# Two more one-time homes for the first experts' weights, asked for during the output projection

## What is computed

```python
for l in range(DEPTH):                                   # 2
    mix = hybrid_mixer(x, w_in[l], ..., w_out[l], cos, sin)
    x = layer_norm(ALPHA * x + mix, ln1_g[l], ln1_b[l])
    ffn = grouped_moe(x, router_w, router_bias, w_gate[l], w_up[l], w_down[l])
    x = layer_norm(ALPHA * x + ffn, ln2_g[l], ln2_b[l])
```

## Time and profile before

| | us |
|---|---|
| median of 3 runs | 2092.38 |
| lowest and highest | 2089.34, 2094.97 |
| the profiled execution | 2092.66 |
| its span | 2090.5 |
| TensorE busy (matmuls) | 1953.0 (93%) |
| VectorE busy | 652.7 (31%) |
| ScalarE busy | 342.4 (16%) |
| mean granted clock | 0.984 |

### The profile page before, as it was taken

The page is one execution under the profiler, slowest core; times in us unless marked ns, Lnnn a source line. Parts: engine busy times, 40 slices in busy tenths (PEclk is TensorE's granted clock), DMA queues, the critical chain, the costliest instruction groups (busy, mean ns, idle before and its releaser), DMA issues.

```text
span 2090.5 us, 26749 instructions
## 1 busy us (share of the span) xinstructions
PE 1953.0 (93%) x10877; PEld 1128.3 (54%) x10877; DVE 652.7 (31%) x1287; ACT 342.4 (16%) x622; POOL 16.8 (1%) x106
## 2 busy tenths in 40 slices
PE   8999999899799999999899999998997999999995
PEld 4688865564544344444347888565645444334442
DVE  1225544441611111111332536545324111111015
ACT  0103220100311011111211132201104111101112
POOL 3000000000000000000000000000000000000000
PEclk9999999999899999999999999999998999999998
DMA  7444342106599999999945433421246999999995
GB/s 234 140 140 142 101 142 100 61 22 221 201 393 422 422 422 422 422 422 422 388 129 164 137 121 124 139 82 61 77 168 260 422 422 422 422 422 422 422 422 237
DMA packets 128831, 539.00 MB, mean 258 GB/s; under 512 B 15856, under 2 KB 20464, under 8 KB 78320
## 3 DMA queue, kind: packets, MB, share of 16 engines
q1 hardware_dynamic: 128752, 537.86, 66.0%
HBM read 535.73 MB, written 2.10 MB: 257 GB/s over the span
## 4 chain that ended last, share of the span: by engine, by line
PE 62%; DMA 31%; DVE 5%; issue 1%; ACT 1%; SPq 1%; DVEq 0%
PE bank L717 19%; PE bank L706 16%; DMA x_t<-in_w_down_dram 16%; DMA x_t<-in_w_up_dram 15%; PE bank L1127 7%; PE bank L1164 4%; PE bank L954 3%; PE bank L741 3%; PE bank L1083 2%; PE bank L652 1%; PE bank L827 1%; PE bank L931 1%; PE bank L842 1%; SPq L579 0%; PE bank L925 0%
## 5 line engine op out<-in xcount | busy, mean ns | idle before, releaser
L706 PE MATMUL bank<-x_t,ring 128*128 128x256 f32 x1536 | 346.2, 384 | 0.0
L706 PEld LDWEIGHTS bank<-x_t,ring 128*128 128x128 f32 x1536 | 291.4, 192 | 50.3 <-issue 11.9
L717 PE MATMUL bank<-ring,x_t 128*128 128x512 f32 (+1 forms) x640 | 258.4, 557 | 1.9 <-DMA ring<-in_w_in_dram 1.9
L1127 PE MATMUL bank<-ring,prob_t 128*64 128x512 f32 x768 | 173.7, 595 | 31.8 <-DMA ring<-in_w_up_dram 31.7
L1937 DVE TENSOR_TENSOR region_a<-bank,region_a 128x512 f32<-128x512 f32 x16 | 11.1, 692 | 580.7 <-PE bank L1127 580.7
L717 PEld LDWEIGHTS bank<-ring,x_t 128*128 128x128 f32 x640 | 120.2, 192 | 116.5 <-issue 109.6
L717 PE MATMUL bank<-ring,mix_acc 128*128 128x512 f32 x384 | 178.4, 602 | 1.5 <-ACT mix_acc L1350 1.5
L1127 PEld LDWEIGHTS bank<-ring,prob_t 128*64 128x64 f32 x768 | 58.1, 137 | 144.0 <-issue 144.0
L1083 PEld LDWEIGHTS bank<-prob_t,x_nat 128*128 128x128 f32 x1024 | 120.7, 199 | 14.4 <-issue 11.4
L1083 PE MATMUL bank<-prob_t,x_nat 128*128 128x128 f32 x1024 | 123.8, 284 | 2.8 <-DVE prob_t L1871 2.8
L1127 PE MATMUL bank<-ring,region_a 128*64 128x512 f32 x512 | 113.4, 595 | 0.0
(11 more groups left out here) (364 smaller groups left out, 1936.0 us busy)
## 6 DMA issues: line engine op xcount, KB each, us to landing
ring<-in_w_gate_dram SPq DMA_DIRECT2D x96, 1024.0 KB, 21.5
ring<-in_w_in_dram SPq DMA_DIRECT2D x80, 1024.0 KB, 5.0
ring<-in_w_up_dram SPq DMA_DIRECT2D x64, 1024.0 KB, 19.1
region_b<-in_w_down_dram SPq DMA_DIRECT2D x48, 1024.0 KB, 21.9
ring<-in_w_out_dram SPq DMA_DIRECT2D x32, 1024.0 KB, 5.1
region_b<-in_w_gate_dram SPq DMA_DIRECT2D x32, 1024.0 KB, 21.1
x_t<-in_w_up_dram SPq DMA_DIRECT2D x32, 1024.0 KB, 23.5
ring<-in_w_down_dram SPq DMA_DIRECT2D x32, 1024.0 KB, 20.6
```

What stands on the lines that cost most here:

```text
L706: m = pe.matmul(b[c // 2][:, (c % 2) * T:(c % 2 + 1) * T], w[:, kk, c * P:(c + 1) * P], xT[:, k, :], start=(k == 0 and c % 2 == 0), stop=( ...
L717: m = pe.matmul(b[t][:, 0:width], lhs[:, k, t * P:(t + 1) * P], w[:, kk, 0:width], start=(k == 0), stop=(k == KC - 1))
L1127: m = pe.matmul(bank[2 + w][rows, :], xg_half[k // 8][:, k % 8 * P + rows.start:k % 8 * P + rows.stop], exp_slot[(n + e) % EXP_SLOTS][:, k ...
```

## The change

Two more pieces of a layer's first pair get homes of their own, `first_slot`, in `region_cd`. For that, the first norm's rows move to `region_a` (`ln1_par`) and its scratch shrinks to one tile of tokens. The homes are renumbered: pieces 0 and 1 of a pair (and 12, 13) now belong to `x_t`, 2 to 4 to `region_b`, 5 to `conv_sq`, 6 to 11 to the ring. Behind the norm rows' requests SyncE now asks for the first pair's pieces 0 and 1 (into `first_slot`) and, after a wait for `o_ready`, for 2 to 5. Its ring pieces are 6 to 11; pieces 12 and 13 wait for the router and go to `x_t`; from 14 on a piece waits for its home. TensorE has the first pair written out, with its own homes for pieces 0 and 1. In the second layer the mixer's pieces wait for the ring pieces at their new places in a pair.

```diff
-        ln_tmp = region_a[:, 0:NT * D].rearrange("p (t d) -> p t d", t=NT)
+        ln_tmp = region_a[:, 0:D]
+        ln1_par = region_a[:, D:3 * D].rearrange("p (g d) -> p g d", g=2)
...
-        exp_slot = [ring[:, n, :] for n in range(RING)]
-        exp_slot += [region_b[:, n * PIECE:(n + 1) * PIECE] for n in range(3)]
-        exp_slot += [conv_sq[:, :], x_t[:, 0:PIECE], x_t[:, PIECE:2 * PIECE]]
+        exp_slot = [x_t[:, 0:PIECE], x_t[:, PIECE:2 * PIECE]]
+        exp_slot += [region_b[:, n * PIECE:(n + 1) * PIECE] for n in range(3)] + [conv_sq[:, :]]
+        exp_slot += [ring[:, n, :] for n in range(RING)]
+        exp_landed = landed[RING:] + landed[:RING]
+        first_slot = [region_cd[:, n * PIECE:(n + 1) * PIECE] for n in range(2)]
...
             def load(n, counted, src):
-                sp.wait_ge(ring_free.sem, counted + (n + 1 + RING if n >= RING else n + 1 + PAIR_PIECES - PAIR_COUNTED))
+                if n >= RING:
+                    sp.wait_ge(ring_free.sem, counted + (n + 1 + RING))
+                elif l and n < PAIR_COUNTED - EXP_SLOTS - RING:
+                    sp.wait_ge(ring_free.sem, counted + (n + 1 + PAIR_PIECES - PAIR_COUNTED + RING))
+                elif l:
+                    sp.wait_ge(down_done.sem, pairs0 * 4)
...
+            def first_pair(counted, experts, l):
+                for n in range(RING, PAIR_PIECES):
+                    if n < EXP_SLOTS - 1:
+                        sp.wait_ge(ring_free.sem, counted + (n + 2))
+                    elif n == EXP_SLOTS - 1:
+                        sp.wait_ge(proj_done.sem, proj_done.at(l, 2 * (N_IN + N_OUT)))
+                    elif n == EXP_SLOTS:
+                        sp.wait_ge(logit_done.sem, logit_done.at(l, 1))
+                    elif n > EXP_SLOTS + 1:
+                        sp.wait_ge(ring_free.sem, counted + (n + 1))
+                    expert_piece(n, experts, exp_slot[n % EXP_SLOTS], exp_landed[n % EXP_SLOTS])
...
                     if (i, j) == (N_IN + 2, 0):
                         sp.wait_ge(to_done.sem, to_done.at(l, 4))
-                        sp.dma_start(ln_par[:, 0, :], row(ln1_g)).then_inc(ln1_loaded.sem, 16)
-                        sp.dma_start(ln_par[:, 1, :], row(ln1_b)).then_inc(ln1_loaded.sem, 16)
+                        sp.dma_start(ln1_par[:, 0, :], row(ln1_g)).then_inc(ln1_loaded.sem, 16)
+                        sp.dma_start(ln1_par[:, 1, :], row(ln1_b)).then_inc(ln1_loaded.sem, 16)
+                        for m in range(2):
+                            expert_piece(m, (l * n_exp, l * n_exp + 1), first_slot[m], first_landed[m])
+                        sp.wait_ge(o_ready.sem, o_ready.at(l, 2))
+                        for m in range(2, RING):
+                            expert_piece(m, (l * n_exp, l * n_exp + 1), exp_slot[m], exp_landed[m])
                 first_e = first + (MIX_PIECES - 1)
-                expert_pair(first_e, pairs0, (l * n_exp, l * n_exp + 1), l)
+                first_pair(first_e, (l * n_exp, l * n_exp + 1), l)
...
-                sp.wait_ge(ln_done.sem, ln_done.at(l, 4))
+                sp.wait_ge(ring_free.sem, first_e + (2 * RING + 2))
                 sp.dma_start(ln_par[:, 0, :], row(ln2_g)).then_inc(affine_loaded.sem, 16)
...
                     def here(n):
                         slot, again = n % EXP_SLOTS, n // EXP_SLOTS
-                        pe.wait_ge(landed[slot].sem, ((uses_e if slot < RING else uses_o) + (again + 1)) * 16)
+                        if first and n < 2:
+                            pe.wait_ge(first_landed[n].sem, first_landed[n].at(l, 1) * 16)
+                            pe.sem_inc(exp_landed[n].sem, 16)
+                        else:
+                            pe.wait_ge(exp_landed[slot].sem, ((uses_o if slot < RING else uses_e) + (again + 1)) * 16)
...
-                with pe.Fori(pairs0, last_pair) as q:
-                    pair_turn(pe.snap(q * 1), False)
-                pair_turn(last_pair, True)
+                pair_turn(pairs0, first=True)
+                with pe.Fori(pairs0 + 1, last_pair) as q:
+                    pair_turn(pe.snap(q * 1))
+                pair_turn(last_pair, last=True)
...
-                    s.do(stt(out=ln_tmp[:, t, :], in0=x_nat[:, t, :], scalar=mean_var[:, t, 0:1], in1=ln_par[:, 0, :],
+                    s.do(stt(out=ln_tmp, in0=x_nat[:, t, :], scalar=mean_var[:, t, 0:1], in1=ln1_par[:, 0, :],
```

More of the change, by code:

```diff
@@ L328, in trunk @@
         landed = [signal(f"landed{i}", 0) for i in range(2 * RING)]
+        first_landed = [signal(f"first_landed{i}", 1) for i in range(2)]
         layer_open = signal("layer_open", 4)
@@ L553, in load, with expert_piece, expert_pair @@
                 sp.dma_start(dst, src).then_inc(landed[n % RING].sem, 16)
-            def expert_pair(counted, turn, experts, l=None):
+            def expert_piece(n, experts, dst, arrived):
+                le = experts[n % 2]
+                if n < 16:
+                    w = (w_gate_v, w_up_v)[n // 8]
+                    src = w[bass.ds(le, 1), :, n % 8 // 2, :].rearrange("a p f -> (a p) f")
+                else:
+                    src = w_down_v[bass.ds(le, 1), :, (n - 16) // 2, :].rearrange("a p d -> (a p) d")
+                sp.dma_start(dst, src).then_inc(arrived.sem, 16)
+            def first_pair(counted, experts, l):
[9 more added lines that the diff above has]
+                    expert_piece(n, experts, exp_slot[n % EXP_SLOTS], exp_landed[n % EXP_SLOTS])
+            def expert_pair(counted, turn, experts):
                 for n in range(PAIR_PIECES):
@@ L560, in expert_pair @@
                         sp.wait_ge(ring_free.sem, counted + (n + 1))
-                    elif l is None and n < EXP_SLOTS - 2:
+                    elif n < EXP_SLOTS - 2:
                         sp.wait_ge(ring_free.sem, counted + (n + 1 + PAIR_PIECES - PAIR_COUNTED))
-                    elif l is None:
+                    else:
                         sp.wait_ge(down_done.sem, turn * 4)
[L565 to L579, removed]
+                    expert_piece(n, experts, exp_slot[n % EXP_SLOTS], exp_landed[n % EXP_SLOTS])
             for l in range(depth):
@@ L1104, in _, with pair_turn, weights @@
                 pairs1 = pe.value_load(pairs[0:1, bass.ds(l + 1, 1)], min_val=n_exp // 2, max_val=depth * TURNS // 2)
-                def pair_turn(q, last):
-                    uses_e = pe.snap((l + 1) * MIX_USES + q * 2)
-                    uses_o = pe.snap(q * 2)
+                def pair_turn(q, first=False, last=False):
+                    uses_e, uses_o = (l + 1) * MIX_USES + q * 2, q * 2
+                    if l or not first:
+                        uses_e, uses_o = pe.snap(uses_e), pe.snap(uses_o)
+                    def weights(n):
+                        return first_slot[n] if first and n < 2 else exp_slot[n % EXP_SLOTS]
                     def here(n):
                         slot, again = n % EXP_SLOTS, n // EXP_SLOTS
-                        pe.wait_ge(landed[slot].sem, ((uses_e if slot < RING else uses_o) + (again + 1)) * 16)
+                        if first and n < 2:
+                            pe.wait_ge(first_landed[n].sem, first_landed[n].at(l, 1) * 16)
+                            pe.sem_inc(exp_landed[n].sem, 16)
+                        else:
+                            pe.wait_ge(exp_landed[slot].sem, ((uses_o if slot < RING else uses_e) + (again + 1)) * 16)
                     for w in range(2):
@@ L1128, in pair_turn @@
                                                   xg_half[k // 8][:, k % 8 * P + rows.start:k % 8 * P + rows.stop],
-                                                  exp_slot[(n + e) % EXP_SLOTS][:, kk * PANEL:(kk + 1) * PANEL],
+                                                  weights(n + e)[:, kk * PANEL:(kk + 1) * PANEL],
                                                   start=(k == 0), stop=(k == KC - 1))
@@ L1164, in pair_turn @@
                                 m = pe.matmul(bank[4 + c][rows, :], hid_t[:, f, rows],
-                                              exp_slot[(n + e) % EXP_SLOTS][:, c * PANEL:(c + 1) * PANEL],
+                                              weights(n + e)[:, c * PANEL:(c + 1) * PANEL],
                                               start=(f == 0), stop=(f == FC - 1))
@@ L1799, in layer_norm @@
                         stt(out=x_nat[:, t, cols].rearrange("p (c q) -> p q c", q=P),
-                            in0=ln_tmp[:, t, :].rearrange("p (q c) -> p q c", c=KC)[:, :, half],
+                            in0=ln_tmp.rearrange("p (q c) -> p q c", c=KC)[:, :, half],
                             scalar=ln_s[:, 1, t:t + 1],
-                            in1=ln_par[:, 1, :].rearrange("p (q c) -> p q c", c=KC)[:, :, half],
+                            in1=ln1_par[:, 1, :].rearrange("p (q c) -> p q c", c=KC)[:, :, half],
                             op0=ALU.mult, op1=ALU.add).then_inc(ln_done.sem, 1)
```

## The result

| | median us | lowest to highest | ratio to before, 95% interval |
|---|---|---|---|
| before (6 runs) | 2092.06 | 2089.34 to 2094.97 | |
| changed (6 runs) | 2100.96 | 2098.7 to 2103.18 | 1.0043 [1.0034, 1.0053] |

The change makes the kernel 8.9 us slower. The profiled execution of the changed kernel took 2103.18 us, the highest of its six, with a span of 2101.4.

The account below looks back on a forecast made before the run. The prediction took TensorE to bound mixer and norm, and the weight stream the experts. Stalls (+3.5, +4.7), clock (+3.0 a layer) and gain (-1.5 a layer) summed to +11.2 us: 2103.6 us, range 2089 to 2109.

Parts of the forecast that it names:

- The late piece: Output projection: six expert pieces ahead delay a weight piece, stalling TensorE 3.5 us in layer 0, 4.7 in layer 1.
- The clock: After each output-projection stall, TensorE's granted clock falls to half for a while, losing 3.0 us a layer.
- rival (a): Output-projection stalls come but the clock holds: +5.2 us, 2097.6 us, within 0.3% of before; chance 0.22.
- The gain: Expert stage: two more homes save 4.97 us of stream, less 3.44 for its later restart: 1.5 us a layer.
- rival (c): No output-projection stall, and two saved pieces count whole at the first pair's restart: 9.9 us gain, 2082.5 us; chance 0.07.
- The rest: Smaller scratch, moved norm rows, renumbered homes, later mixer requests and the written-out first pair together cost nothing.
- The total: Whole kernel: +5.0 us in layer 0 and +6.2 in layer 1, together +11.2, giving 2103.6 us.

Follow-up runs that it names:

- filler: The changed kernel with six needless products a layer on TensorE ahead of its wait for the late output-projection piece: 2097.97 us, 1.003 against before.
- five ahead: The changed kernel with the sixth early expert request moved behind the output-projection pieces, five staying ahead: 2092.47 us, 1.0001 against before.
- restart: The changed kernel with all six requests behind the projection and the extra homes used twice in the first pair: 2085.86 us, 0.997 against before.
- Twelve homes: The changed kernel with six requests behind the projection and without the two extra homes: 2090.65 us, 0.9994 against before.
- six behind: The changed kernel with all six early expert requests moved behind the remaining output-projection pieces: 2086.21 us, 0.9974 against before.
- two ahead: The changed kernel with only the two requests for the new homes ahead of the output-projection pieces, four behind: 2086.96 us, 0.9979 against before.
- norm rows behind: The changed kernel with its six expert requests still ahead, but the two norm rows moved behind all mixer pieces: 2085.15 us, 0.9971 against before.

## Why the prediction was right, and where it was off

The sign, the size (+11.2 forecast, +8.9 measured, interval 7.1 to 11.1) and the mechanism came out; term by term:

- **The late piece.** Forecast stalls of 3.5 and 4.7 us, together 8.2; measured stands of 5.10 and 3.16, with the 0.27 us each 5.4 and 3.4, together 8.8. The cause is shown from both sides: by moving the six, four of them, one of them, and the norm rows instead. Layer by layer it was off by 1.9 us one way and 1.3 the other, and that the sum is so near is partly luck: I took each layer's landing from one execution, and it varies. Counted from the first norm row's request, (13,1) landed 16.6 us later than before in layer 0 and 13.5 in layer 1; their mean, 15.05, is the forecast 14.9. TensorE's need after 48 records was exact.
- **The clock.** Forecast 3.0 us each. The 48 records behind the stands took 23.68 - 20.87 = 2.8 and 22.56 - 20.87 = 1.7 us longer, 4.5 in all instead of 6.0. Behind the longer stand 5.7 us of work ran at 0.50, behind the shorter one 3.4. That it is a cost of its own is shown by the filler in layer 0; rival (a), the clock holding, is what five ahead looks like. The sum without a clock term, +5.2 us, lies below the measured interval. The Trainium skill (TensorE: Matmul & The Clock Gate, section What's actually happening) puts the ramp's cost below 1% of a typical span. The trace agrees, as 4.5 us are 0.2% of this one; but in a difference of 0.4% they are half.
- **The gain.** Forecast 1.5 us a layer; measured 1.4 in layer 0 (2.55 in layer 1, against that long stage of the kernel before), and 1.4 between twelve and fourteen homes. The full 4.97 us of rival (c) does not come, and the restart kernel takes back 1.1 of the 3.44 that the late restart eats. In its timeline the request behind pieces 14 and 15 comes 6.86 us after theirs (584.26 against 577.40), longer than two pieces last.
- **The rest.** Forecast nought. Twelve homes bears it out within its interval. The mixer pieces asked for later in layer 1 cost nothing: from the last expert wait of layer 0 to the projection's rest of layer 1 it is 476.22 us before and 476.21 after. (In the other seven profiles this stretch takes 475.82 to 478.10 us, so that two executions agree so closely is chance.)
- **The total.** The forecast stood 2.6 us too high. By the profiles the terms are 8.8 of stalls and 4.5 of clock, less 2.8 for the homes: +10.5 instead of +11.2, the clock 1.5 us too high and the late pieces 0.6 too low. The runs say +8.9 with an interval up to 11.1, so the remaining 1.6 us are not clear of the spread; 0.3 is the other median of the kernel before.
- **A reading.** Slices 12 to 20 and 30 to 39 do not all run at 422 GB/s, as the prediction has it: 422 stands in seven slices of the first expert stage and in eight of the second, and the slices at their edges show 393 and 388, 260 and 237. No term rests on it.

Open: why six behind gains 5.5 us where the homes explain 2.8. In its profile norm and routing add 2.8, but one execution does not show that for eleven. The other two without stalls and with the late restart, two ahead and norm rows behind, gain 4.4 and 6.1 us, with intervals that reach down to 2.5 and 3.8. All kernels with the rest of the change but five ahead come out 1 to 3 us under the sum of their stalls, clock and homes, and twelve homes, 1.3 us under before, leans the same way. So some part that was put at nought (the renumbered homes, the written-out pair, the norm rows' place) may give a little; no run separates it.

## What to carry to other kernels

An early request is free only as long as everything asked for behind it in the same queue still lands in time: work out how long the next needed transfer has in hand, and divide by the time of one transfer. Here it was 10 to 11 us, four pieces, and the change put six there; with five, two short stands were left, and with four more than before none. Put into such a gap what is needed next, and move whatever is needed last (here the norm rows) to the end.

Two more buffers do not save two transfers when the stream stands until a buffer comes free: ask at which release it restarts.

## What had not been expected

- SyncE can be held in the act of asking. With some eight transfers outstanding, two requests of the changed kernel that began at 479.47 were through only 14.06 us later (5.36 us the first, 8.7 the second), where requests of the same pieces took 0.4 to 0.7 in the kernel before. That kernel has a longer one near the end of its layer 0. SyncE's timeline of the changed kernel, a window from 482 to 489, then of the kernel before, 1013 to 1020:

```profile
479.47 14.06 SPq L562 DMA_DIRECT2D ring<-in_w_out_dram  x2
```

```profile
1012.19 17.69 SPq L553 DMA_DIRECT2D ring<-in_w_in_dram  x1
```

  No second stall followed here, since the stream was full meanwhile. But the second of the two requests began only at 484.87, when the first was through; so a small request behind them would be held as well, which no run here tries. What holds them is not shown.
- The norm and routing, a stretch of broken work, takes between 29.6 and 32.8 us in these nine profiles, though eight of the nine kernels have the same code there. It goes with the granted clock: 0.83 in the two stretches of six behind (29.68 and 29.62 us), 0.78 where it takes 30.9 to 31.1, 0.73 at 31.14, 0.67 or 0.68 at 31.2 to 31.7, and 0.64 at 32.78. Differences of 1 to 2 us between single executions of this kernel mean nothing unless that stretch is read apart.
